# Routing of a two-layer decoder trunk: expert places counted on token rows, the sort ahead of the gates' spread

## The reference, cut to what matters

```
scores = sigmoid(h @ w_router)                  # tokens x 64
biased = scores + router_bias
# 4 of 8 groups of experts by the sum of their two best, then the 8 best experts in them
w = scores at idx;  w = 2.5 * w / sum(w)        # the gates
routed = sum over experts e of gate[e] * (silu(h @ w_gate[e]) * (h @ w_up[e])) @ w_down[e]
shared = (silu(h @ sh_gate) * (h @ sh_up)) @ sh_down
```

## Time and profile before

| | us |
|---|---|
| three timed runs | 1547.74, 1553.97, 1555.4 (median 1553.97) |
| the profiled execution | 1548.17 |
| its span, first to last instruction | 1546.3 |
| busy: TensorE, VectorE, ScalarE, GpSimd | 1439.7, 649.5, 342.0, 244.7 |
| mean granted clock of TensorE | 0.968 of 2.4 GHz |

### The profile page before, as it was taken

The page is one execution under the profiler, slowest core; times in us unless marked ns, Lnnn a source line. Parts: engine busy times, 40 slices in busy tenths (PEclk is TensorE's granted clock), DMA queues, the critical chain, the costliest instruction groups (busy, mean ns, idle before and its releaser), DMA issues. The chain is left out here.

```text
span 1546.3 us, 24294 instructions
## 1 busy us (share of the span) xinstructions
PE 1439.7 (93%) x9414; PEld 849.9 (55%) x9414; DVE 649.5 (42%) x1461; ACT 342.0 (22%) x712; POOL 244.7 (16%) x323
## 2 busy tenths in 40 slices
PE   8999989999899999897999889989999989979996
PEld 6888768887445545353545467864543333424442
DVE  2767448632632433242433358053234323414324
ACT  3756454220410111010111030141101111101111
POOL 5779625200100000000000000011000000000000
PEclk9999999899999999998999989999999999989998
DMA  8669461049599999999999973498999999999994
GB/s 282 218 190 243 174 173 47 2 164 365 208 417 422 423 420 424 424 421 425 421 425 421 409 281 129 169 392 336 417 424 423 421 425 422 425 421 424 422 423 183
DMA packets 105679, 512.37 MB, mean 331 GB/s; under 512 B 36932, under 2 KB 42116, under 8 KB 68444
## 3 DMA queue, kind: packets, MB, share of 16 engines
q1 hardware_dynamic: 95740, 481.75, 78.7%
q0 software_dynamic: 9824, 29.05, 5.0%
HBM read 508.85 MB, written 17.10 MB: 340 GB/s over the span
## 5 line engine op out<-in xcount | busy, mean ns | idle before, releaser
L1855 PE MATMUL banks<-upper,e_xgT 128*64 128x512 f32 (+1 forms) x880 | 195.1, 609 | 3.5 <-DMA upper<-in_moe_gate_up 2.1
L2064 DVE TENSOR_TENSOR e_ac<-e_sl,banks 128x256 f32<-128x256 f32 x54 | 22.8, 421 | 405.8 <-ACT e_sl L1982 405.8
L346 PE MATMUL banks<-hT,dense_ring 128*128 128x272 f32 x768 | 183.3, 396 | 5.3 <-DMA dense_ring<-in_w_in 5.2
L1444 POOL DMA_INDIRECT x_xg<-rows_dram,x_idx x54 | 53.8, 996 | 824.7 <-DVE x_idx L1436 808.6
L346 PEld LDWEIGHTS banks<-hT,dense_ring 128*128 128x128 f32 x768 | 145.8, 191 | 39.0 <-DMA dense_ring<-in_w_in 5.4
L1855 PE MATMUL banks<-dense_ring,e_xgT 128*64 128x512 f32 (+1 forms) x288 | 134.5, 622 | 34.7 <-issue 34.7
L1855 PE MATMUL banks<-experts,e_xgT 128*64 128x512 f32 (+1 forms) x720 | 159.3, 604 | 1.1 <-DMA experts<-in_moe_gate_up 0.9
L1982 ACT ACTIVATE e_sl<-banks 128x256 f32<-128x256 f32 x54 | 20.8, 385 | 491.2 <-PE banks L1855 491.2
L1855 PEld LDWEIGHTS banks<-upper,e_xgT 128*64 128x64 f32 (+1 forms) x880 | 65.0, 131 | 91.0 <-issue 91.0
L1875 PE MATMUL banks<-x_sg,route_consts 128*128 128x272 f32 x432 | 104.4, 393 | 0.5 <-DVE acc L2051 0.5
L1873 PE MATMUL banks<-route_consts,x_sg 128*128 128x512 f32 x216 | 97.6, 594 | 0.8 <-DVE acc L2048 0.8
(11 more groups left out here) (450 smaller groups left out, 2061.1 us busy)
## 6 DMA issues: line engine op xcount, KB each, us to landing
upper<-in_moe_gate_up SPq DMA_DIRECT2D x45, 2048.0 KB, 27.9
experts<-in_moe_gate_up SPq DMA_DIRECT2D x36, 2048.0 KB, 27.1
upper<-in_moe_down SPq DMA_DIRECT2D x43, 1024.0 KB, 25.5
experts<-in_moe_down SPq DMA_DIRECT2D x43, 1024.0 KB, 26.4
dense_ring<-in_moe_down SPq DMA_DIRECT2D x38, 1024.0 KB, 25.5
dense_ring<-in_moe_gate_up SPq DMA_DIRECT2D x18, 2048.0 KB, 19.1
dense_ring<-in_w_in SPq DMA_DIRECT2D x47, 512.0 KB, 4.8
upper<-in_moe_gate_up SPq DMA_DIRECT2D x20, 1024.0 KB, 15.0
```

What stands on the lines that cost most here:

```text
L346: mm = pe.matmul(ps[g % 4][:, 0:T], slot[:, n % SLOTS_IN, c, :], hT[:, c, :], start=(c == 0), stop=(c == DC - 1))
L1444: pool.indirect_dma_start(out=ex["xg"][:, i % 2, :], out_offset=None, in_=mem["rows_dram"], in_offset=bass.IndirectOffsetOnAxis(ap=ex["idx ...
L1855: mm = pe.matmul(gub[e * n:(e + 1) * n, :], xgT[:, i % 2, c, e * n:(e + 1) * n], gate_up_weights(mem, j)[:, c, :], start=(c == 0), stop=(c ...
L2064: dve.tensor_tensor(ac[:], sl[:], gub[:, FF:], ALU.mult).then_inc(mul, 1)
```

## The change

Ranks are counted with tokens in partitions, in place of experts: `place_ps` holds for each tile the products of `after` with `sel` of this and the earlier tiles, and VectorE writes (rank + 1) x `sel` back into `sel`. The turned `sel` gives places by expert in a bank of its own (`row_places_ps`), from which VectorE takes the counts directly and ScalarE copies the places. The turned `sg2` now serves for the gates alone. `select_unit` for units 0 and 1 stands in the normalisation. On TensorE the keys' product comes ahead of the spread places, and the spread gates come behind the sort. On VectorE both units are located behind the ranks and scattered at the very end; the places are lifted with two operations in place of one. Three semaphores are added and one dropped.

```
--- before.py
+++ after.py
@@ -1457,7 +1457,7 @@
         sem = inner.enter_context(Signals(nc, mem["numbers"]["odd"], f"r{layer}_"))
         sb = lambda name, shape, dt=F32: inner.enter_context(nc.sbuf_tensor(f"r{layer}_{name}", shape, dt))
         bank = mem["bank"]
-        sums, sqs, lg_ps, bias_ps, sc_ps, rank_ps, both_ps = (bank[b] for b in (4, 5, 6, 7, 0, 5, 3))
+        sums, sqs, lg_ps, bias_ps, sc_ps, place_ps, row_places_ps, both_ps = (bank[b] for b in (4, 5, 6, 7, 0, 5, 4, 3))
         row_ps = [bank[b] for b in (1, 2, 3, 7, 1, 2)]
         sh_ps = [bank[b] for b in (6, 4, 5, 3)]
         spread_ps = ((bank[1], bank[2]), (bank[7], bank[0]))
@@ -1476,7 +1476,7 @@
         m8 = sb("m8", [P, NT * GROUPS, 8])
         gs, g8, gm = (sb(n, [P, NT, GROUPS]) for n in ("gs", "g8", "gm"))
         t8, ws = sb("t8", [P, NT, 8]), sb("ws", [P, NT])
-        maskT = sb("maskT", [E, W])
+        lifted = sb("lifted", [E, W])
         cm, key, rank, extra = (sb(n, [E, 1]) for n in ("cm", "key", "rank", "extra"))
         keys, above, at_rank = (sb(n, [E, E]) for n in ("keys", "above", "at_rank"))
         row, rank2 = sb("row", [1, E]), sb("rank2", [P, 1])
@@ -1490,8 +1490,8 @@
         weighed, biased, bias_in, logits, logit_in, scored = (sem(n) for n in (
             "weights_scaled", "bias_summed", "bias_in", "logits_summed", "logits_scaled", "scored"))
         score_turned, rows_t, rows_c, stored = sem("scores_turned"), sem("rows_turned"), sem("rows_copied"), mem["rows_stored"]
-        step_s, selected, gated, ranked, masked, placed = (sem(n) for n in (
-            "step", "selected", "gated", "ranked", "mask_in", "placed"))
+        step_s, selected, gated, ranked, located, placed, gates_spread, counted = (sem(n) for n in (
+            "step", "selected", "gated", "ranked", "places_by_token", "placed", "gates_spread", "counted"))
         keyed, spread, placed_by, sorted_, maxed = (sem(n) for n in (
             "keys_ready", "keys_spread", "ranks_ready", "sorted", "count_ready"))
         warmed, ordered, asked = sem("table_held"), sem("order_ready"), sem("gather_asked")
@@ -1558,26 +1558,36 @@
                     turn_rows(i)
                 pe.wait_ge(selected, 1)
                 for tt, (t0, n) in enumerate(tiles):
-                    mm = pe.matmul(rank_ps[0:E, 0:W], sel[0:n, tt, :], after[0:n, tt, 0:W],
-                                   start=(tt == 0), stop=(tt == NT - 1))
+                    for src, (_, held) in enumerate(tiles[:tt + 1]):
+                        mm = pe.matmul(place_ps[0:n, tt * E:(tt + 1) * E], after[0:held, src, t0:t0 + n], sel[0:held, src, :],
+                                       start=(src == 0), stop=(src == tt))
+                mm.then_inc(ranked, 1)
+                pe.wait_ge(located, 1)
+                for tt, (t0, n) in enumerate(tiles):
+                    mm = pe.transpose(row_places_ps[0:E, t0:t0 + n], sel[0:n, tt, :], ident[0:n, 0:n])
                 mm.then_inc(ranked, 1)
                 pe.wait_ge(gated, 1)
                 pe.wait_ge(rows_c, 3)
                 for tt, (t0, n) in enumerate(tiles):
                     mm = pe.transpose(both_ps[:, t0:t0 + n], sg2[0:n, tt].rearrange("p q e -> p (q e)"), ident[0:n, 0:n])
                 mm.then_inc(ranked, 1)
-                pe.wait_ge(placed, 2)
-                pe.wait_ge(rows_c, 2 * NT)
-                for i in range(2):
-                    spread_unit(pe, mem, ex, i, spread_ps[i], W)
                 pe.wait_ge(mem["expert_consts"], 16 * len(EXPERT_CONSTS))
                 pe.wait_ge(keyed, 1)
                 pe.matmul(key_ps[0:E, 0:E], ones[0:E, 0:E], keys[:], start=True, stop=True).then_inc(spread, 1)
-                pe.wait_ge(masked, 1)
+                pe.wait_ge(placed, 1)
+                pe.wait_ge(rows_c, 2 * NT)
+                pe.wait_ge(ex["unit_selected"], 2)
+                for i in range(2):
+                    pe.matmul(spread_ps[i][0][:, 0:W], ex["selw"][0:E, i], pg[0:E, 0:W], start=True, stop=True).then_inc(
+                        ex["rows_broadcast"], 1)
+                pe.wait_ge(placed, 2)
                 pe.wait_ge(placed_by, 2)
                 pe.matmul(sort_ps[:, 2 * E:2 * E + 1], twice, rank[:], start=True, stop=True)
                 pe.matmul(sort_ps[0:1, 0:E], number, at_rank[:], start=True, stop=True)
                 pe.matmul(sort_ps[0:1, E:2 * E], cm[:], at_rank[:], start=True, stop=True).then_inc(sorted_, 1)
+                for i in range(2):
+                    pe.matmul(spread_ps[i][1][:, 0:W], ex["selw"][E:, i], pg[E:, 0:W], start=True, stop=True).then_inc(
+                        gates_spread, 1)
                 pe.wait_ge(gu_ready, 32 * (layer + 1))
                 for j in range(ahead):
                     shared_half(pe, mem, ex, hN, sh_ps[j], j)
@@ -1610,11 +1620,13 @@
                     src = row_ps[i][0:n, :].rearrange("p (c q r) -> p c q r", c=4, r=DC)
                     dst = row_tile(tt)[0:n].rearrange("p (r c q) -> p c q r", r=DC, c=DC)[:, 4 * half:4 * half + 4]
                     act.copy(dst, src).then_inc(rows_c, 1)
-                act.wait_ge(ranked, 2)
-                act.copy(maskT[:], both_ps[0:E, 0:W]).then_inc(masked, 1)
+                act.wait_ge(counted, 1)
+                act.copy(pg[0:E, 0:W], row_places_ps[0:E, 0:W]).then_inc(placed, 1)
+                act.wait_ge(ranked, 3)
                 act.copy(pg[E:, 0:W], both_ps[E:, 0:W]).then_inc(placed, 1)
                 for i in range(2):
-                    gates_in(act, ex, i, spread_ps[i], W)
+                    act.wait_ge(gates_spread, i + 1)
+                    act.copy(ex["gsb"][:, i], spread_ps[i][1][:, 0:W]).then_inc(ex["gates_in"], 1)
                 for m in range(min(ahead, FC)):
                     shared_silu(act, mem, ex, sh_ps, m, W)
 
@@ -1631,6 +1643,10 @@
                     dve.wait_ge(logits, c + 1)
                     dve.tensor_tensor(hN[:, c, :], hN[:, c, :], rstd[:], ALU.mult).then_inc(scaled, 1)
 
+                dve.wait_ge(mem["expert_consts"], 16 * len(EXPERT_CONSTS))
+                fixed = mem["unit_first"]
+                for i in range(2):
+                    select_unit(dve, mem, ex, i, fixed[:, len(UNITS) + i:len(UNITS) + i + 1])
                 dve.wait_ge(biased, 1)
                 dve.tensor_copy(bias[:], bias_ps[0:E, 0:1]).then_inc(bias_in, 1)
                 dve.wait_ge(sd_ready, 1)
@@ -1677,32 +1693,25 @@
                 dve.wait_ge(selected, 1)
                 link(dve.tensor_tensor(gt, sc, sel, ALU.mult))
                 link(dve.tensor_reduce(ws[:], gt, AX_X, ALU.add))
+                dve.wait_ge(ranked, 1)
+                dve.scalar_tensor_tensor(out=sel, in0=place_ps[:, 0:NT * E].rearrange("p (t e) -> p t e", t=NT), scalar=1.0,
+                                         in1=sel, op0=ALU.add, op1=ALU.mult).then_inc(located, 1)
                 link(dve.reciprocal(ws[:], ws[:]))
                 link(dve.tensor_scalar(ws[:], ws[:], SCALE, None, ALU.mult))
                 dve.tensor_tensor(gt, gt, ws[:].unsqueeze(2).broadcast_to([P, NT, E]), ALU.mult).then_inc(gated, 1)
-                dve.wait_ge(mem["expert_consts"], 16 * len(EXPERT_CONSTS))
-                fixed = mem["unit_first"]
-                for i in range(2):
-                    select_unit(dve, mem, ex, i, fixed[:, len(UNITS) + i:len(UNITS) + i + 1])
-                dve.wait_ge(masked, 1)
-
-                dve.scalar_tensor_tensor(out=pg[0:E, 0:W], in0=rank_ps[0:E, 0:W], scalar=1.0, in1=maskT[:],
-                                         op0=ALU.add, op1=ALU.mult).then_inc(placed, 1)
-                dve.wait_ge(placed, 2)
-                link(dve.tensor_reduce(cm[:], pg[0:E, 0:W], AX_X, ALU.max))
+                dve.wait_ge(ranked, 2)
+                dve.tensor_reduce(cm[:], row_places_ps[0:E, 0:W], AX_X, ALU.max).then_inc(counted, 1)
+                dve.wait_ge(counted, 1)
                 link(dve.scalar_tensor_tensor(out=key[:], in0=cm[:], scalar=float(E), in1=key_off, op0=ALU.mult,
                                               op1=ALU.add))
                 dve.tensor_scalar(keys[:], ident[0:E, 0:E], key[:, 0:1], None, ALU.mult).then_inc(keyed, 1)
-                locate_unit(dve, mem, ex, 0, spread_ps[0], W)
                 dve.wait_ge(spread, 1)
                 dve.scalar_tensor_tensor(out=above[:], in0=key_ps[0:E, 0:E], scalar=key[:, 0:1], in1=ones[0:E, 0:E],
                                          op0=ALU.is_gt, op1=ALU.mult, accum_out=rank[:]).then_inc(placed_by, 1)
                 dve.wait_ge(placed_by, 1)
                 dve.tensor_scalar(at_rank[:], ranks, rank[:, 0:1], None, ALU.is_equal).then_inc(placed_by, 1)
-                locate_unit(dve, mem, ex, 1, spread_ps[1], W)
                 for i in range(2):
-                    scatter_unit(dve, mem, ex, i, spread_ps[i], W)
-                link(dve.tensor_scalar(extra[:], rank[:], PAIR_RANKS - 0.5, float(SLOTS // 2), ALU.is_gt, ALU.mult))
```

(10 more changed lines are left out.)

25 lines of the change are left out of this document (6 added, 19 removed).

## The result

The changed kernel is slower: 1557.2 us (median of 20 runs, 1553.15 to 1563.69) against 1552.72 of the kernel before (20 runs, 1547.74 to 1559.94); ratio 1.0028, 95% interval 1.0016 to 1.0041, so 4.4 us with an interval of 2.5 to 6.4. I had forecast 1550.6 and a range up to 1557.0. The miss of 6.6 is made of three parts: 1.4 from the base (1552.72 for the 1551.3 that I started from), 0.7 of gain that did not come, and 4.5 of loss, by the medians.

What follows compares the result with a forecast made beforehand. TensorE's queue was taken to end the routing blocks, with DMA and TensorE both full in the expert stages behind. +0.37 (layer 0) and -1.03 (layer 1) gave -0.7 on 1551.3: 1550.6 us, range 1545.5 to 1557.0.

Steps and rivals of the forecast that it cites:

- Where TensorE's queue sets the block's end: Routing stages: TensorE's queue is the path to the block's end; gathers have 1.3 us of slack on their indices.
- That a shift of the routing's end moves the whole time: Expert stages behind routing: untouched by the change, so an earlier or later start reaches the end in full.
- Ranking 1.35 + 0.15: Layer 0, TensorE: twelve narrow ranking instructions take 1.35 us, plus 0.15 until the result can be read, at 402.3.
- Indices: Layer 0: unit 0's index, located behind the ranks, is ready at 406.15, needed at 406.8; cost zero.
- Order: Order ready earlier: layer 0's first load gains 0.3 us at most, layer 1's fifth expert comes up to 0.95 earlier.
- Layer 0, +0.37: TensorE, layer 0: gates' spread alone behind the sort starts the shared half at 407.15 against 406.78, +0.37 us.
- rival D: Layer 0 loses its full clock: +3.4 us on the forecast's -0.7, so +2.7; chance 0.05.
- Layer 1, -1.03: TensorE, layer 1: gap-free work brings the clock's rise to 1047.05, shared half ends at 1051.1 instead of 1052.13, -1.03 us.
- rival A: Gates' spread behind the sort slows TensorE's queue: +0.37 in layer 0, +0.4 in layer 1, +0.8 in all; chance 0.25.
- Rival B: Gates' spread is free, overlapping the sort's tail: -0.3 and -0.5 us, in all -1.5; chance 0.13.
- Rival C: Layer 0's indices come too late, at 407.6 past 406.8, delaying gather 0: +0.1 to +0.8 us; chance 0.07.
- E: Nothing arrives, since the weights' stream sets the end whatever unit 0 does: 0.0 us; chance 0.10.

Runs made afterwards that it cites:

- the best kernel: Changed kernel with the spread in pairs, products of constants in TensorE's waits, and SyncE waiting for the second gather: 1546.42 us, ratio 0.9967 to the kernel before.
- Filled before, with the later load: Kernel before with products of constants in TensorE's waits and SyncE waiting for the second gather before loading the fifth expert: 1547.0 us, ratio 0.9974.
- the filled changed kernel: Changed kernel with products of constants, result unused, in TensorE's waits: 1554.45 us, ratio 1.0015 to the kernel before.
- The companions: Changed kernel with a product of constants on the array's other half beside each spread product: 1551.82 us, ratio 0.9995 to the kernel before.

## Why the prediction was wrong, by its own steps

Where TensorE's queue sets the block's end: right. In every trace without a late gather unit 0 starts 4.7 to 7.5 us behind the shared half's start, which is its length and about 1 us of block border, at either clock. The one exception is layer 1 of the best kernel, with its 2.3 of wait for the gather.

That a shift of the routing's end moves the whole time: right, as a mean. The execution's time less unit 0's start in layer 1 is 494.4 to 496.0 in 18 of the 20 traces, whatever the distances were, and 497.8 and 498.0 in the two with a late gather there. From unit 0 in layer 0 to the selection in layer 1 they take 625.1 to 630.6, so a single execution can hide a shift of some us. The distances of both layers summed give 26.1 before (mean of four traces), 31.6 after (three): +5.5, inside the measured 2.5 to 6.4. Filled before, with the later load: 22.8, so -3.3 against a measured -4.0. The best: 20.9, so -5.2 against -5.1. These last two are one trace each, and that they come out so near is partly luck.

Ranking 1.35 + 0.15: measured 1.42, read by VectorE 1.59 behind the selection. Keys' product 3.70 behind the selection in layer 0, measured 3.89, and 3.78 in layer 1, measured 3.76. Indices: ready at 407.57 in layer 0 instead of 406.15, since the products ahead of them ran at half clock; gather 0 started 7.3 behind the selection, 0.5 later than before, hidden behind the shared half. Order: SyncE's load came 0.98 us behind the gather in layer 1 instead of 1.66, as foreseen, without loss here.

Layer 0, +0.37: failed. I priced it from rows at 1.00. As a price at that clock it is good: in layer 1 of the filled changed kernel, at 1.00, the places' spread took 0.97 (1045.78 to 1046.75), and I had 0.94. But at 0.50 the two spreads took 2.0 and 2.1. The shared half started 9.2 us behind the selection, not 6.4, and the layer lost 4.6 in this trace, 4.1 in the means (12.3 to 16.4). This was rival D, with a price of 3.4 and a chance of 0.05. The price was low, because the 5.25 that I took for a slow shared half is from a row whose last 2.1 us ran at 1.00; with a later rise it took 5.41 to 6.43. The chance was the error: I had one trace in which layer 0 held its clock and took it for the rule. The unchanged kernel loses it in one of four traces and the changed one lost it in all four, for a reason that the runs make likely but do not show.

Layer 1, -1.03: failed, and this is the step as I put it: "the same 4.1 put the rise at 1047.05". TensorE's rows had no gap from the keys' product on, and the rise still came 10.6 us after it. The old rise had followed 4.1 us in which the shared half, with all 128 rows of the array, had run for 3.1; I read "no gap" where the row also said full height. The companions turn the same queue into one whose clock returns about 3 us earlier, counted from the shared half's start. What I got was rival A with a larger price: +1.4 in layer 1 in the means, against +0.4.

Rival B did not occur: in layer 0 the gates' spread starts 0.35 behind the start of the last sort product (two instructions, 0.41), not beside it. The Trainium skill, TensorE: Matmul & The Clock Gate (Part 3, The mechanism), says that products of different row groups overlap; the traces agree for products issued next to each other, as the companions in the third trace, which start at 408.19 and 408.20. Nothing here shows it for the sort's tail. Rival C came in part and hidden, E did not occur. The loss of 0.3% was told apart from no change, finer than the 0.5% that I had put as the limit.

## What to carry to other kernels

Taking apart two products that run beside each other on two halves of the array cost twice here: the second's own time (0.97 for four products at full clock, 2.1 at half), and a clock that came back about 3 us later, as a queue of products on one half at a time did not bring it back as one that used both halves did. Ask of a gap-free stretch of TensorE how high and how wide its products are, not only how busy it is. Before pricing a stage from one trace, take two or three: whether its clock holds may vary from one execution of a kernel to the next, and here that alone, 5.5 us, was larger than every term of the change.

## What the hardware showed unasked

TensorE ran 5.1 us without a gap over 0.1 us (1048.07 to 1053.17) on products of 64 rows, some with one moving column, and the clock stayed at 0.50 for 5.5 us more of full products. Constants in otherwise idle time, with the load moved, took the kernel before from a mean clock of 0.965 to 0.968 over its runs and gave 4.0 us back. In these traces a gather landed late when a load on another queue came close behind it: 0.1 us in the issue of 2 MB of weights (0.85 against 0.96 behind the gather's start) parts landings of 8.6 us and more (3 stages) from ones of 5.4 and less (37 stages).
